# Norms of a two-layer diffusion trunk cut into pieces by tokens, and a weight transpose moved into a projection

## The chip, the cores and the metric

The kernel runs on one core of one Trainium2 chip. A core has five engines that run side by side and meet only at semaphores: TensorE (PE, matrix products), VectorE (DVE), ScalarE (ACT), GpSimdE (POOL) and SyncE (SP), which here only issues DMAs. The metric is the device time of one execution in microseconds.

## The reference

Two blocks of 128 tokens with 1024 features go through two layers: block 0 (the code's t = 0) is a context prompt, block 1 (t = 1) a set of noisy latents. Each block has its own conditioning vector, from which a modulation (shift, scale, gate) is computed for each norm. Cut to what matters here:

```python
h = rms_norm(x, norm_mix[l]) * (1.0 + sc1) + sh1
out = even_mixer(h, ...)             # layer 0: attention and gated DeltaNet
out = odd_mixer(h, ...)              # layer 1:
#   z = gelu(h @ w_in); u, v = split(z)
#   v = layer_norm(v)
#   mixed = einsum("gpq,bnqgc->bnpgc", w_s, v) + b_s
#   out = (u * mixed) @ w_out
x = x + g1 * out
h = rms_norm(x, norm_ffn[l]) * (1.0 + sc2) + sh2
x = x + g2 * hier_moe(h, ...)        # router, then 2 of 32 experts a token
```

All weights are float32 and stream in from HBM: 288 MB are read. `w_s` (the spatial weights) are four 128x128 matrices that mix tokens; the product on PE needs them transposed.

## The kernel before

The residual stream `xT` and the normalised stream `hT` lie with features on the partitions, as [128, 8 tiles, 2 blocks, 128 tokens]. Every engine's program is written out by hand in the order in which it runs, and engines wait on counting semaphores: nothing is scheduled. Weights come in slots of 2 MB, eleven of them (five in `ring`, six in `scratch`, the code's `more`). SP issues the loads in a fixed order; each waits until the slot's previous user is done (`used`, or for one slot `v_mix`, line 668). From the fourth of eleven expert passes on, SP must also know which experts the routing chose (line 703).

**A router norm** (`moe`, lines 1276, 1862 and 2370) goes block by block. DVE adds half of a block's out-projection to `xT` (`residual`, line 2348, four tiles at a time) and signals `v_x`; ACT squares these four tiles (line 1625), signals `a_sq`; PE sums the squares with a product against ones (`mean_square_of`, line 881); ACT takes the root (lines 1617 and 1620); DVE multiplies all eight tiles of the block by it (line 2378) and signals `v_xn`. Then DVE modulates tiles 0 to 3 (line 2069) and ACT tiles 4 to 7 (line 1630). PE waits for both (`h_ready`, line 889) and runs the router products (line 1286). For block 0 all of this lies beside the out-projection of block 1; for block 1 there is little else for PE.

**The norm ahead of layer 1's in-projection** (`norm`, lines 1638 and 2073) takes both blocks at once and is cut by tiles: DVE normalises tiles 0 to 3 of both blocks (line 2085, 1024 columns), DVE modulates them for block 0 while ACT does for block 1; then the same with tiles 4 to 7. The in-projection on PE first computes v, block 0 with all eight tiles, then block 1 (line 1536); its first product waits for the first half, its fifth tile for the second.

**The spatial weights** are loaded by ACT's DMA queue behind that norm (line 1956, with three more small loads). PE transposes them (line 1557) after the last u product of the in-projection (line 1549), ACT copies the result to `wsT` (line 1980) after its last gelu and a table load (`roots()`), and PE mixes (line 1563) when the copy (`a_ws`) and the layer norm (`v_ln`) are there. DVE follows each quarter of the mixing with an addition and a product (lines 2680 and 2682), and the out-projection (line 1262) waits for the first two.

## Time and profile before

| | |
|---|---|
| median of three timed runs | 843.4 us (842.76 to 843.53) |
| profiled execution, its own time | 846.99 us |
| its span | 845.0 us |
| PE busy | 785.5 us, 93% |
| DVE / ACT busy | 321.5 / 166.5 us |
| DMA | 291.47 MB, mean 345 GB/s, hardware queue 87.3% of 16 engines' span |
| mean granted PE clock | 0.973 |

The span is what the profiler saw of the core's work; the time of the execution is 2.0 us longer. Times in the views count from the span's start. Durations below all come from this one execution. A matmul in float32 appears as two PE instructions, so that sixteen products of 128x128 read as x32. The granted clock is a share of full speed: 1.00 or 0.50.

### The profile page before, as it was taken

Reading aid. Unit: us, or ns where it says so; the run is one execution under the profiler, and the core shown is the slowest. Engines: PE = TensorE matmul, PEld = TensorE weight load, DVE = VectorE, ACT = ScalarE, POOL = GpSimd, SP = SyncE. Lnnn points to the kernel's source line nnn. Section 1 sums busy time; section 2 is a strip of 40 time slices with the busy share of each in tenths; the row PEclk is TensorE's granted clock in tenths of the full one; section 3 lists DMA queues with packets and bytes.
Section 4 is the critical chain, followed back from the end, with each engine's and each line's share of the span. In section 5 each row is a group of like instructions: output and inputs, shape, how many; then the busy total and the mean of one; then the engine's idle time right before and its main releaser. Section 6 shows DMA issues by size and latency. Waiting matters only on the chain.

```text
span 845.0 us, 15981 instructions
## 1 busy us (share of the span) xinstructions
PE 785.5 (93%) x6910; PEld 524.4 (62%) x6910; DVE 321.5 (38%) x687; ACT 166.5 (20%) x323; POOL 12.3 (1%) x17
## 2 busy tenths in 40 slices
PE   3999999998999999999977989989999999998697
PEld 3788568677898655556542444679865545664244
DVE  1155467653414433433332340223353344333224
ACT  3112411323203111111100141040321111111013
POOL 0000001020000000000000000000000000000000
PEclk9999999999999999999998999999999999999798
DMA  9999779493899599999999999996549999999993
GB/s 342 387 371 386 254 261 353 147 344 104 274 390 399 222 414 363 362 417 415 420 415 411 400 387 385 389 409 243 200 147 417 384 361 417 416 419 415 413 402 144
DMA packets 97879, 291.47 MB, mean 345 GB/s; under 512 B 11833, under 2 KB 14991, under 8 KB 87567
## 3 DMA queue, kind: packets, MB, share of 16 engines
q1 hardware_dynamic: 86960, 284.32, 87.3%
q10 hardware_dynamic: 10847, 6.11, 2.5%
q8 instruction: 56, 0.92, 0.4%
q14 instruction: 16, 0.13, 0.0%
HBM read 288.30 MB, written 2.10 MB: 344 GB/s over the span
## 4 chain that ended last, share of the span: by engine, by line
PE 74%; SPq 11%; DMA 7%; DVE 2%; ACT 2%; issue 2%; ACTq 1%; DVEq 0%
PE psum L1360 7%; PE psum L1262 7%; PE psum L905 7%; PE psum L1335 6%; PE psum L1345 6%; PE psum L1392 5%; PE psum L858 5%; PE psum L965 5%; DMA scratch<-in_w_exp_up 5%; SPq L742 5%; PE psum L1536 4%; PE psum L1549 3%; PE psum L1403 3%; SPq L761 2%; PE psum L1027 2%
## 5 line engine op out<-in xcount | busy, mean ns | idle before, releaser
L1345 PE MATMUL psum<-scratch,hT 128*32 128x512 f32 (+1 forms) x384 | 77.0, 647 | 16.5 <-DMA ring<-in_w_exp_up 8.7
L1335 PE MATMUL psum<-scratch 128*128 128x128 f32 x704 | 82.9, 276 | 0.9 <-DVE scratch L2478 0.9
L1335 PEld LDWEIGHTS psum<-scratch 128*128 128x128 f32 x704 | 80.5, 192 | 1.3 <-issue 1.2
L1345 PE MATMUL psum<-ring,hT 128*32 128x512 f32 (+1 forms) x288 | 67.7, 619 | 5.1 <-DMA scratch<-in_w_exp_up 5.1
L905 PE MATMUL psum<-hT,ring 128*128 128x256 f32 x256 | 57.8, 383 | 1.1 <-DVE hT L2069 0.7
L1403 PEld LDWEIGHTS psum<-const,scratch 128*128 128x128 bf16 x480 | 45.1, 97 | 21.5 <-issue 13.6
L1403 PE MATMUL psum<-const,scratch 128*128 128x256 bf16 x480 | 55.9, 272 | 1.5 <-DVE scratch L2494 1.5
L1345 PEld LDWEIGHTS psum<-scratch,hT 128*32 128x32 f32 (+1 forms) x384 | 21.0, 122 | 54.1 <-issue 54.1
L905 PEld LDWEIGHTS psum<-hT,ring 128*128 128x128 f32 x256 | 47.9, 190 | 9.6 <-DVE hT L2069 2.0
L2487 DVE TENSOR_SCALAR hT<-psum,const 128x512 f32<-128x512 f32 x22 | 16.5, 751 | 95.1 <-PE psum L1392 93.6
L1903 ACT ACTIVATE scratch<-psum 128x256 f32<-128x256 f32 x22 | 8.4, 383 | 211.4 <-PE psum L1345 124.8
L1360 PE MATMUL psum<-scratch,hT 128*64 128x512 f32 (+1 forms) x208 | 42.7, 594 | 0.6 <-DMA scratch<-in_w_exp_up 0.6
L965 PE MATMUL psum<-ring,hT 128*128 128x512 f32 x96 | 42.6, 597 | 0.0
L2498 DVE TENSOR_TENSOR scratch<-psum,scratch 128x256 f32<-128x256 f32 x22 | 9.3, 425 | 84.3 <-ACT scratch L1903 84.3
L858 PE MATMUL psum<-ring,condT 128*2 128x128 f32 x1280 | 40.4, 282 | 0.0
L1392 PE MATMUL psum<-scratch,const 128*32 128x512 f32 (+2 forms) x248 | 40.1, 596 | 0.0
L858 PEld LDWEIGHTS psum<-ring,condT 128*2 128x2 f32 x1280 | 32.5, 88 | 7.4 <-issue 4.1
L1345 PEld LDWEIGHTS psum<-ring,hT 128*32 128x32 f32 (+1 forms) x288 | 17.9, 118 | 30.4 <-issue 30.4
L1360 PE MATMUL psum<-ring,hT 128*64 128x512 f32 (+1 forms) x176 | 35.7, 594 | 0.8 <-DMA ring<-in_w_exp_up 0.8
L1392 PE MATMUL psum<-ring,const 128*32 128x512 f32 (+2 forms) x216 | 32.8, 596 | 0.0
L1536 PE MATMUL psum<-ring,hT 128*128 128x512 f32 x64 | 29.7, 624 | 2.2 <-ACT hT L1630 2.2
L965 PEld LDWEIGHTS psum<-ring,hT 128*128 128x128 f32 x96 | 17.8, 190 | 20.8 <-issue 20.7
...
## 6 DMA issues: line engine op xcount, KB each, us to landing
...
```

What stands on the lines that cost most here:

```text
L742: sp.dma_start(slot(s)[:, at:at + 1024], w[e][:, 1024 * kh:1024 * kh + 1024]).then_inc(full[s], 16)
L858: last = mm(bank[mbank[g]][32 * m:32 * m + NB, at:at + P], condT[:, :, k], w[:, k, m * P:(m + 1) * P], start=(k == 0), stop=(k == KT - 1))
L905: last = mm(out[:, c2 * T:(c2 + 1) * T], w[:, k, m * P:(m + 1) * P], hT[:, k, :, :], start=(k == 0 and k1 == KT), stop=(k == k1 - 1), skip ...
L965: last = mm(bank[b], hT[:, k, t, :], w[:, k, :], start=(k == 0), stop=(k == KT - 1))
L1262: last = mm(bank[2 * t + m // 4][:, (m % 4) * P:(m % 4 + 1) * P], w[m // 4][:, k, (m % 4) * P:(m % 4 + 1) * P], hT[:, k, t, :], start=(k = ...
L1335: last = mm(bank[b][:, k * P:(k + 1) * P], hrow[:, t, half * 4 + k, :], Pm[:, t, :], start=(t == 0), stop=(t == 1))
L1345: last = mm(bank[0][i * m:(i + 1) * m, :], xg[:, k, i * m:(i + 1) * m], w[e][:, k, :, :], start=(k == 0), stop=(k == KT - 1))
L1360: last = mm(bank[0][i * m:(i + 1) * m, :], xg[:, 4 * kh + k, i * m:(i + 1) * m], w[i // 2][:, i % 2, k, :, :], start=(kh == 0 and k == 0), ...
L1392: last = mm(bank[1 + half][i * m:(i + 1) * m, :], hidT[:, a, i * m:(i + 1) * m], slot(slots[e // 2])[:, base:base + 512], start=(a == 0), ...
L1403: last = mm(bank[4 + k // 2][:, (k % 2) * T:(k % 2 + 1) * T], y3[:, j, k, :], ohT, start=False, stop=True, skip_group_check=True)
L1536: last = mm(bank[4 + 2 * j + t], hT[:, k, t, :], w[:, k, :], start=(k == 0), stop=(k == KT - 1))
L1549: last = mm(bank[b][:, (m % 2) * T:(m % 2 + 1) * T], w[:, k, m * P:(m + 1) * P], hT[:, k, :, :], start=(k == 0), stop=(k == KT - 1))
```

## The change

There are three parts. The norms are cut by tokens and tiles: in `norm` DVE normalises four tiles of one block (512 columns), four times, and each engine modulates two of these four tiles, DVE the first two and ACT the last two; in `moe` the block's normalisation becomes two of 512 columns, tiles 4 to 7 (ACT's) first. The last half of the residual of block 1 is signalled twice, after two tiles and after four; ACT squares each pair by itself and PE waits for each. The transposes of the spatial weights stand on PE in front of the second u chunk of the in-projection, and ACT's copy ahead of the gelu of that chunk. The counts of the semaphores follow (`SQ0`, `H0`).

```diff
@@ -79,7 +79,8 @@
 MOE_SLOTS = PASS_AT[NPASS]
 
 
-SQ0 = [None, None, 0, 4, 8, 12]
+SQ0 = [None, None, 0, 5, 9, 14]
+H0 = [None, 0, 2, 4, 8]
 MS0 = [None, None, 0, 2, 3, 5]
 
 
@@ -881,15 +882,15 @@
             def mean_square_of(n, sq, b, t):
 
                 for k in range(KT):
-                    if k % 4 == 0:
-                        pe.wait_ge(S.a_sq, SQ0[n] + 2 * t + k // 4 + 1)
+                    if k in (0, 4) or (t == 1 and k == 6):
+                        pe.wait_ge(S.a_sq, SQ0[n] + 2 * t + (0, 0, 1, 2)[k // 2] + 1)
                     last = mm(bank[b][:, t * P:(t + 1) * P], ones, sq[:, k, t * P:(t + 1) * P], start=(k == 0), stop=(k == KT - 1))
                 last.then_inc(S.t_ms, 1)
 
             def h_ready(n, i):
 
-                pe.wait_ge(S.v_h, 2 * (n - 1) + i + 1)
-                pe.wait_ge(S.a_h, 2 * (n - 1) + i + 1)
+                pe.wait_ge(S.v_h, H0[n] + i + 1)
+                pe.wait_ge(S.a_h, H0[n] + i + 1)
 
             mod_chunk(0, 0)
             mod_chunk(0, 2)
@@ -1531,8 +1532,8 @@
                 w = slot_kn(s)
                 for t in range(NB):
                     for k in range(KT):
-                        if j == 0 and t == 0 and k % 4 == 0:
-                            h_ready(3, k // 4)
+                        if j == 0 and k % 4 == 0:
+                            h_ready(3, 2 * t + k // 4)
                         last = mm(bank[4 + 2 * j + t], hT[:, k, t, :], w[:, k, :], start=(k == 0), stop=(k == KT - 1))
                     if t == 0:
                         last.then_inc(S.t_v, 1)
@@ -1543,6 +1544,11 @@
                 w = slot_kn(s)
                 if j == 1:
                     pe.wait_ge(S.v_mod, M_B + 1)
+                    pe.wait_ge(S.ld_router, 16 * 10)
+                    pe.wait_ge(S.a_gv, 4)
+                    for g in range(4):
+                        last = nc.tensor.transpose(bank[4][:, g * P:(g + 1) * P], wsp[:, g, :], ident)
+                    last.then_inc(S.t_ws, 1)
                 for m in range(4):
                     b = 2 * j + m // 2
                     for k in range(KT):
@@ -1551,11 +1557,6 @@
                     if m == 1:
                         last.then_inc(S.t_u, 1)
                 used(last)
-            pe.wait_ge(S.ld_router, 16 * 10)
-            pe.wait_ge(S.a_gv, 4)
-            for g in range(4):
-                last = nc.tensor.transpose(bank[4][:, g * P:(g + 1) * P], wsp[:, g, :], ident)
-            last.then_inc(S.t_ws, 1)
             pe.wait_ge(S.a_ws, 1)
             for t in range(NB):
                 pe.wait_ge(S.v_ln, t + 1)
@@ -1638,9 +1639,10 @@
             def norm(n, b, l, shift):
 
                 root_mean(n, b, 0, NB)
-                for half in range(2):
-                    act.wait_ge(S.v_xn, 2 * (n - 2) + half + 1)
-                    modulate(n, l, shift, 4 * half, 4 * half + 4, 1)
+                for t in range(NB):
+                    for half in range(2):
+                        act.wait_ge(S.v_xn, 4 * (n - 2) + 2 * t + half + 1)
+                        modulate(n, l, shift, 4 * half + 2, 4 * half + 4, t)
 
             def mod_row(g):
 
@@ -1862,11 +1864,11 @@
             def moe(l):
                 n = 2 * l + 2
                 for t in range(NB):
-                    for half in range(2):
-                        act.wait_ge(S.v_x, 4 * l + 2 * t + half + 1)
-                        squares(n, sqm, 4 * half, 4 * half + 4, t, t + 1)
+                    for i, (k0, k1) in enumerate([(0, 4), (4, 8)] if t == 0 else [(0, 4), (4, 6), (6, 8)]):
+                        act.wait_ge(S.v_x, 5 * l + 2 * t + i + 1)
+                        squares(n, sqm, k0, k1, t, t + 1)
                     root_mean(n, 5, t, t + 1)
-                    act.wait_ge(S.v_xn, 2 * (n - 2) + t + 1)
+                    act.wait_ge(S.v_xn, 4 * (n - 2) + 2 * t + 1)
                     modulate(n, l, 3 * KT, 4, KT, t)
                 tokens_rows(l, 0)
                 tokens_rows(l, 1)
@@ -1975,9 +1977,9 @@
                 A(uT[:, 2 * b:2 * b + 2, :].rearrange("p k n -> p (k n)"), bank[b], ACT.Gelu_apprx_tanh).then_inc(S.a_gelu, 1)
                 if b == 1:
                     layer_norm_scale()
+                    act.wait_ge(S.t_ws, 1)
+                    A(wsT[:, :, :].rearrange("p g n -> p (g n)"), bank[4], ACT.Copy).then_inc(S.a_ws, 1)
             roots()
-            act.wait_ge(S.t_ws, 1)
-            A(wsT[:, :, :].rearrange("p g n -> p (g n)"), bank[4], ACT.Copy).then_inc(S.a_ws, 1)
 
             moe(1)
             moe_experts(1)
@@ -2074,17 +2076,17 @@
 
                 dve.wait_ge(S.a_rstd, MS0[n] + 2)
                 dve.wait_ge(S.v_a, 4)
-                for half in range(2):
-                    k = 4 * half
-                    normalise(k)
-                    dve.wait_ge(S.v_xn, 2 * (n - 2) + half + 1)
-                    modulate(n, l, shift, k, k + 4, 0)
-
-            def normalise(k):
-
-                V.tensor_tensor(hT[:, k:k + 4, :, :].rearrange("p k t n -> p k (t n)"),
-                                xT[:, k:k + 4, :, :].rearrange("p k t n -> p k (t n)"),
-                                bcast_mid(rstd[:, :], 4), ALU.mult).then_inc(S.v_xn, 1)
+                for t in range(NB):
+                    for half in range(2):
+                        k = 4 * half
+                        normalise(t, k)
+                        dve.wait_ge(S.v_xn, 4 * (n - 2) + 2 * t + half + 1)
+                        modulate(n, l, shift, k, k + 2, t)
+
+            def normalise(t, k):
+
+                V.tensor_tensor(hT[:, k:k + 4, t, :], xT[:, k:k + 4, t, :],
+                                bcast_mid(rstd[:, t * P:(t + 1) * P], 4), ALU.mult).then_inc(S.v_xn, 1)
 
             dve.wait_ge(S.v_xt, 3)
             for half in range(2):
@@ -2357,6 +2359,8 @@
                     for m in range(4 * half, 4 * half + 4):
                         last = V.scalar_tensor_tensor(xT[:, m, t, :], bank[2 * t + half][:, (m % 4) * P:(m % 4 + 1) * P],
                                                       modT[:, l * MT + 2 * KT + m, t:t + 1], xT[:, m, t, :], ALU.mult, ALU.add)
+                        if t == 1 and m == 5:
+                            last.then_inc(S.v_x, 1)
                     last.then_inc(S.v_x, 1)
 
             def add_scaled(src, b, at):
@@ -2375,8 +2379,9 @@
                     residual(["out0", "out1"][l], l, t)
                     dve.wait_ge(S.a_rstd, MS0[n] + t + 2)
                     dve.wait_ge(S.v_a, 5)
-                    V.tensor_tensor(hT[:, :, t, :], xT[:, :, t, :], bcast_mid(rstd[:, t * P:(t + 1) * P], KT), ALU.mult).then_inc(S.v_xn, 1)
-                    dve.wait_ge(S.v_xn, 2 * (n - 2) + t + 1)
+                    normalise(t, 4)
+                    normalise(t, 0)
+                    dve.wait_ge(S.v_xn, 4 * (n - 2) + 2 * t + 2)
                     modulate(n, l, 3 * KT, 0, 4, t)
                 dve.wait_ge(S.t_lg, 2 * l + 2)
                 link(V.tensor_tensor(lg, bank[0][:, 0:72].rearrange("p (t n) -> p t n", t=2),
```

The norm ahead of the in-projection on DVE, before (`hT<-xT,rstd` is a normalisation, `hT<-hT,mulA,modT` a modulation of one tile of one block, L2059 the modulation vectors of the next norm):

```order
L2085 TENSOR_TENSOR hT<-xT,rstd 128x1024 [waits v_a,a_rstd]
L2069 TENSOR_SCALAR hT<-hT,mulA,modT 128x128 [waits v_xn]
L2069 TENSOR_SCALAR hT<-hT,mulA,modT 128x128 x3
L2085 TENSOR_TENSOR hT<-xT,rstd 128x1024
L2069 TENSOR_SCALAR hT<-hT,mulA,modT 128x128 [waits v_xn]
L2069 TENSOR_SCALAR hT<-hT,mulA,modT 128x128 x3
L2059 TENSOR_TENSOR modT<-psum,cols 128x16 [waits t_mod]
```

The same norm on DVE in the change, in which L2088 is the normalisation and L2071 the modulation:

```order
L2088 TENSOR_TENSOR hT<-xT,rstd 128x4x128 [waits v_a,a_rstd]
L2071 TENSOR_SCALAR hT<-hT,mulA,modT 128x128 [waits v_xn]
L2071 TENSOR_SCALAR hT<-hT,mulA,modT 128x128
L2088 TENSOR_TENSOR hT<-xT,rstd 128x4x128
L2071 TENSOR_SCALAR hT<-hT,mulA,modT 128x128 [waits v_xn]
L2071 TENSOR_SCALAR hT<-hT,mulA,modT 128x128
L2088 TENSOR_TENSOR hT<-xT,rstd 128x4x128
L2071 TENSOR_SCALAR hT<-hT,mulA,modT 128x128 [waits v_xn]
L2071 TENSOR_SCALAR hT<-hT,mulA,modT 128x128
L2088 TENSOR_TENSOR hT<-xT,rstd 128x4x128
L2071 TENSOR_SCALAR hT<-hT,mulA,modT 128x128 [waits v_xn]
L2071 TENSOR_SCALAR hT<-hT,mulA,modT 128x128
```

Two normalisations of 1024 columns with four modulations each have become four of 512 with two each; the first modulation stands behind half of the columns.

The end of the in-projection on PE, before (`hT,ring` and `hT,scratch` are the two u chunks, `const,scratch` the transposes against the identity, L1563 the mixing):

```order
L1549 MATMUL psum<-hT,ring 128x256 [waits slot_full2]
L1549 MATMUL psum<-hT,ring 128x256 x31
L1549 MATMUL psum<-hT,scratch 128x256 [waits v_mod,slot_full10]
L1549 MATMUL psum<-hT,scratch 128x256 x31
L1557 MATMUL psum<-const,scratch 128x128 [waits a_gv,ld_router]
L1557 MATMUL psum<-const,scratch 128x128 x3
L1563 MATMUL psum<-scratch 128x128 [waits v_ln,a_ws]
L1563 MATMUL psum<-scratch 128x128 x7
L1563 MATMUL psum<-scratch 128x128 [waits v_ln]
L1563 MATMUL psum<-scratch 128x128 x7
L1262 MATMUL psum<-hT,scratch 128x128 [waits slot_full9,v_mix,a_gelu]
```

The same stretch of PE in the change, in which L1550 is the transpose, L1555 the u product and L1564 the mixing:

```order
L1555 MATMUL psum<-hT,ring 128x256 [waits slot_full2]
L1555 MATMUL psum<-hT,ring 128x256 x31
L1550 MATMUL psum<-const,scratch 128x128 [waits ld_router,a_gv,v_mod,slot_full10]
L1550 MATMUL psum<-const,scratch 128x128 x3
L1555 MATMUL psum<-hT,scratch 128x256 x32
L1564 MATMUL psum<-scratch 128x128 [waits v_ln,a_ws]
L1564 MATMUL psum<-scratch 128x128 x7
L1564 MATMUL psum<-scratch 128x128 [waits v_ln]
L1564 MATMUL psum<-scratch 128x128 x7
L1263 MATMUL psum<-hT,scratch 128x128 [waits slot_full9,v_mix,a_gelu]
```

The four transposes, with their waits for ACT's small loads (`ld_router`) and for the last gelu of v (`a_gv`), have moved ahead of the 32 products of the second chunk; the mixing now stands directly behind these.

ACT in the same place, before (L1975 is the gelu of u, L1980 the copy):

```order
L1951 ACT_TABLE_LOAD
L1975 ACTIVATE scratch<-psum 128x512 [waits t_u]
L1975 ACTIVATE scratch<-psum 128x512 [waits used]
L1596 ACT_TABLE_LOAD
L1980 ACTIVATE scratch<-psum 128x512 [waits t_ws]
L1625 ACTIVATE scratch<-xT 128x4x128 [waits v_x] x2
```

The same stretch of ACT in the change, in which L1977 is the gelu and L1981 the copy:

```order
L1953 ACT_TABLE_LOAD
L1981 ACTIVATE scratch<-psum 128x512 [waits t_ws]
L1977 ACTIVATE scratch<-psum 128x512 [waits t_u]
L1977 ACTIVATE scratch<-psum 128x512 [waits used]
L1597 ACT_TABLE_LOAD
L1626 ACTIVATE scratch<-xT 128x4x128 [waits v_x] x2
```

The copy has moved from behind the last gelu and a table load to a place ahead of the third gelu.

## Rows read from the trace of the kernel before

**Rows 1.** The page, part 4: the chain that ended last, shares of the span by engine.
```profile
PE 74%; SPq 11%; DMA 7%; DVE 2%; ACT 2%; issue 2%; ACTq 1%; DVEq 0%
```

**Rows 2.** The chain in order of time (start us, us, what), its two longest DMA pieces.
```profile
465.79 15.35 DMA scratch<-in_w_exp_up
...
803.97 15.62 DMA ring<-in_w_exp_up
```

**Rows 3.** Windows: engines' busy us (count), granted clock, DMA share, GB/s; before each expert stage.
```profile
275.00:283.00 8.00, 7.06 (x117) 6.34 (x110) 6.17 (x33) 1.87 (x3) 0.00 (x0) 1.00 0.02 7
...
610.00:620.00 10.00, 9.13 (x158) 7.98 (x162) 6.81 (x39) 3.73 (x7) 0.00 (x0) 0.83 0.01 3
```

**Rows 4.** Timeline, first router norm (start us, us, engine line op out<-in xcount [idle <-releaser]).
```profile
252.94 1.95 PE L886 MATMUL psum<-scratch,const 128*128 128x128 f32 x16
...
262.72 2.35 PE L886 MATMUL psum<-scratch,const 128*128 128x128 f32 x16
...
265.85 1.23 DVE L2378 TENSOR_TENSOR hT<-xT,rstd 128x1024 f32<-128x1024 f32 x1 [2.65 <-ACT rstd L1620]
...
267.11 1.65 ACT L1630 ACTIVATE hT<-hT,modT,mulA 128x128 f32<-128x128 f32 x4 [1.29 <-DVE hT L2378]
267.11 1.12 DVE L2069 TENSOR_SCALAR hT<-hT,mulA,modT 128x128 f32<-128x128 f32 x4
...
268.91 2.13 PE L1286 MATMUL psum<-wrt,hT 128*128 128x36 f32 x16 [0.47 <-ACT hT L1630]
```

**Rows 5.** Timeline, norm ahead of the in-projection and the in-projection's two v halves.
```profile
502.45 1.23 DVE L2085 TENSOR_TENSOR hT<-xT,rstd 128x1024 f32<-128x1024 f32 x1 [3.37 <-ACT rstd L1620]
503.72 1.65 ACT L1630 ACTIVATE hT<-hT,modT,mulA 128x128 f32<-128x128 f32 x4 [1.29 <-DVE hT L2085]
...
505.51 15.67 PE L1536 MATMUL psum<-ring,hT 128*128 128x512 f32 x32 [2.19 <-ACT hT L1630]
...
522.97 14.00 PE L1536 MATMUL psum<-ring,hT 128*128 128x512 f32 x32
```

**Rows 6.** Line 697, loads issued at 485.6 and 488.1: first in-projection chunk, issue to landing.
```profile
DMA to landing us min/median/max: 12.6/14.3/16.1
```

**Rows 7.** Lines 2682 and 1630, every instruction (ns min/median/max, first and last start).
```profile
L2682 DVE TENSOR_TENSOR hT<-hT,scratch x4: 691/692/693, 570.3 to 574.5; 128x512 f32<-128x512 f32 x4
...
L1630 ACT ACTIVATE hT<-hT,modT,mulA x32: 477/478/496, 23.2 to 609.5; 128x128 f32<-128x128 f32 x32
```

**Rows 8.** Timeline, between the in-projection and the out-projection of layer 1.
```profile
565.47 1.28 ACT L1596 ACT_TABLE_LOAD   x1
566.76 0.60 ACT L1980 ACTIVATE scratch<-psum 128x512 f32<-128x512 f32 x1
...
567.41 5.47 PE L1563 MATMUL psum<-scratch 128*128 128x128 f32 x32 [2.16 <-ACT scratch L1980]
569.56 0.69 DVE L2680 TENSOR_TENSOR hT<-psum,scratch 128x512 f32<-128x512 f32 x1 [8.77 <-PE psum L1563]
...
572.72 21.61 PE L1262 MATMUL psum<-hT,scratch 128*128 128x128 f32 x192
```

**Rows 9.** Windows of one microsecond: granted clock is the third number from the end.
```profile
500.00:501.00 1.00, 1.00 (x6) 0.89 (x5) 0.00 (x0) 0.00 (x0) 0.00 (x0) 1.00 1.05 385
506.50:507.50 1.00, 1.00 (x2) 0.34 (x1) 0.62 (x3) 1.00 (x3) 0.00 (x0) 0.50 1.05 387
567.50:568.50 1.00, 1.00 (x5) 1.00 (x6) 0.00 (x0) 0.00 (x0) 0.00 (x0) 0.50 1.07 426
...
767.00:768.00 1.00, 1.00 (x12) 0.31 (x8) 0.97 (x2) 0.00 (x0) 0.00 (x0) 1.00 1.00 401
```

**Rows 10.** Timeline of PE, a short and a longer wait elsewhere.
```profile
499.36 2.10 PE L878 MATMUL psum<-scratch,const 128*128 128x256 f32 x9 [0.97 <-issue]
...
766.31 0.59 PE L1345 MATMUL psum<-scratch,hT 128*32 128x512 f32 x1 [2.42 <-DMA ring<-in_w_exp_up]
```

**Rows 11.** Line 1959, the last of ACT's four small loads, issued at 507.5: issue to landing.
```profile
DMA to landing us min/median/max: 12.1/12.1/12.1
```

## The prediction

> **What bounds the kernel now.** I read the chain of waits first: PE holds 74% of it, SP's DMA issues 11%, DMA 7% [rows 1]. Which share matters where shows in the same chain in order of time: its long DMA pieces stand at the end of the two expert stages, to 481.1 and to 819.6 [rows 2]. So an expert stage ends when its weights have landed, 2 MB slot after slot. The next question is what starts that stream. The windows ahead of both expert stages answer it: from 275 to 283 the DMA engines are 2% busy, from 610 to 620 1% [rows 3]. Every slot is full there, and no load goes out until routing has chosen experts or PE has freed a slot. An expert stage is therefore a block of nearly fixed length that starts when routing ends, and a microsecond saved ahead of routing is saved at the end, in PE's part of the block and in DMA's. The edits all lie ahead of one or both of these points, so I read the timeline there for what PE waits for.
>
> **1. Router norms (in both layers), second block of tokens.** PE runs the second mean square as 16 instructions in 2.35 us, where the first took 1.95 with nothing to wait for; then DVE normalises 1024 columns in 1.23, ACT's four modulations take 1.65 and DVE's four 1.12, and PE starts the router products 1.80 us after both engines began, having sat idle 0.47 [rows 4].
> - With the residual half signalled after two tiles, ACT squares 256 columns twice instead of 512 once. PE reaches tile 4 at about 263.6, when the first pair is there, and the last pair comes before tile 6: the mean square should cost 1.95, so 0.40 is saved.
> - A normalisation of 512 columns takes 0.69 by the nearest row, an operation of the same shape and operand kinds [rows 7]. ACT can start after the first: 0.69 instead of 1.23, and would end 0.54 earlier. DVE now has 0.69 + 0.69 + 1.12 = 2.50 where it had 1.23 + 1.12 = 2.35, so DVE ends last. The pass was 1.23 + 1.65 and gaps = 2.91 (265.85 to 268.76); it becomes 2.50 and gaps of 0.05 = 2.55. Saved: 0.36.
> - PE itself could start the router products 0.47 + 0.40 = 0.87 earlier at most; the sum of 0.76 lies inside that. I take 0.75 a layer, **1.5 in all**. Bounds: 0.35 a layer if the two short normalisations eat the second part, 0.87 if they overlap.
>
> **2. Norm ahead of the in-projection.** Before, PE waits 2.19 us: DVE normalises four tiles of both token blocks (502.45, 1.23), then ACT's four modulations of block 1 run 503.72 to 505.37, and PE starts at 505.51 although its first products read block 0 alone [rows 5]. After: 0.69 for 512 columns, then two modulations on each engine; ACT's take 0.48 + 0.39 (its four take 1.65, so 0.39 apart) = 0.87. Ready at 502.45 + 0.69 + 0.04 + 0.87 = 504.05, PE at 504.2: 1.31 earlier. What is late next? The second half of the first weight chunk was issued at 488.1 and took 16.1 us, so it landed at 504.2 [rows 6]; the two nearly tie. I take **1.2**. The later pieces are ready one per 1.3 us or so (0.69 + 0.60), while PE needs 3.5 for each, and stay covered. Bounds: 0.9 (landing a little late) to 1.31.
>
> The Trainium skill, page "VectorE: DVE Perf Modes", section "The TRN2 errata — SBUF-src ops pay a fixed extra latency per instruction", speaks against pieces: many small operations pay a fixed cost each. The trace shows it: 2 x 0.69 against 1.23, 0.15 for each split [rows 5, 7]. By that rule alone, with DVE's total deciding, this norm would end 0.3 us later and the router norms 0.15; the trace puts DVE's total on the path only in the router norms, where it is in my sum.
>
> **3. The clock after that wait.** The in-projection's first 32 matmuls took 15.67 us, the next 32 of the same shape 14.00 [rows 5]; at 506.5 the granted clock was 0.50, that is 1.2 instead of 2.4 GHz [rows 9]. It fell right after the wait of 2.19. A wait of 0.97 just before left it at 1.00 [rows 9, 10]. The new wait is 2.19 - 1.2 = 1.0. So I count 15.67 - 14.00 = **1.65** as saved. Bounds: 0 and 1.67.
>
> **4. Spatial weights.** Before, ACT has a table load (1.28) and then the copy (0.60) between the last in-projection product and the mixing; PE is idle 2.16 [rows 8]. Now both transposes and copy happen about ten microseconds earlier, in a stretch where PE is busy and ACT idle; the four transposes cost PE the same wherever they stand. PE goes on at once: **2.1**. The mixing then took 5.47 for 32 instructions at clock 0.50, again after a wait over 2 us [rows 8, 9]; at the out-projection's pace (21.61 for 192, 0.113 each) it is 3.6, 1.85 less. But DVE follows each quarter with two operations of 0.69 [rows 7, 8]: first quarter done about 1.25 after the start, then four operations with gaps, 2.85, then 0.15 to PE: the out-projection starts 4.25 after the mixing instead of 572.72 - 567.41 = 5.31. So the clock gives **1.05** here, bounds 0 and 1.7. The moved-up transposes wait for four small loads issued by ACT at 506 to 507.5; the last landed 12.1 later, at 519.6 [rows 11], over 25 us before PE asks.
>
> **Sum.** 1.5 + 1.2 + 1.65 + 2.1 + 1.05 = 7.5 us. The profiled execution took 847.0 (span 845.0 and 2.0 around it), so it would take 839.5. The three timed runs had a median of 843.4, 3.6 shorter; the saved waits are compute waits and should be in those too, so I subtract the same: **835.9**.
>
> **The rivals.**
> - *Waits go, the clock gives nothing* (it does not fall in the timed runs, or falls elsewhere after the change). For: the timed runs are 3.6 shorter than the profiled one, about what two clock drops cost; and after a wait of 2.42 at 766.31 the clock was still 1.00 [rows 9, 10]. Against: both waits on these places show it. Without items 3 and the clock part of 4, 7.5 - 2.7 = 4.8: 838.6. Beside it: the Trainium skill, "TensorE: Matmul & The Clock Gate", section "What's actually happening", says that how many matmuls run slow differs from execution to execution of one kernel; by that the 2.7 would be there in some executions and absent in others.
> - *The weights decide in the in-projection.* PE, 2.9 us ahead, meets the landing of its chunks. For: rows 6, a tie already for the first chunk. Against: only this chunk is that close, and its stream itself starts 0.75 earlier. If items 2 and 3 vanish: 7.5 - 2.85 = 4.65, and 838.8.
> - *The expert stream hides all.* If the DMA stream had been full through routing, nothing of this would reach the end: 843.4. The 2% and 1% of rows 3 speak against it.
> - *Slower: a stall inside the second in-projection.* The transposes now stand in front of that projection's second chunk on PE, with 12 us of products, the mixing and everything behind them. If the four small loads land later than about 547, PE stops; each microsecond of lateness costs one, and the clock 1.67 more once the wait is long. It overcomes the 7.5 from about 553 on, 46 us after issue, and at 50 us would give 843.4 - 7.5 + 10.5 + 1.7 = 848. Against: 12.1 us of landing [rows 11], in a stretch where the DMA engines were already saturated.
>
> **How the numbers follow.** Forecast 0.62 (own range 834.4 to 837.4: half of each bound), clock gives nothing 0.20, weights decide 0.08, stream hides all 0.04, stall 0.03, and 0.03 for more than the sum, where the clock also stays up in the first router stage. A difference of 0.2%, 1.7 us, is about what can be told from none. Faster by more than that: 0.62 + 0.20 + 0.08 + 0.03 = 0.93, of which I give back 0.02 for small sums going wrong together: 0.91. Within: 0.05. Slower: 0.04. The range runs from 834.0 (all upper bounds) to 840.0 (waits alone, with the lower bounds of 1 and 2).
>
> **What would show it.** Router norm: mean square of block 1 in about 1.95, first normalisation to router products 2.7 instead of 3.1, DVE ending last. In-projection: a wait near 1.0, the first 32 matmuls in 14.0 at clock 1.00. Mixing: directly behind the in-projection, about 4 us at clock 1.00, with DVE releasing the out-projection. Idle DMA engines still ahead of both expert stages, and the stages' lengths unchanged. Wrong: a clock of 0.5 in either place, an in-projection released by DMA, expert stages that grow by what was saved ahead of them.

## The result, and the profile after

| | before | changed |
|---|---|---|
| median of the timed runs beside each other, us | 843.66 (7 runs, 842.76 to 851.66) | 838.33 (7 runs, 834.74 to 843.53) |
| profiled execution, us | 847.0 | 837.6 |
| its span, us | 845.0 | 835.8 |

The ratio of the runs beside each other is 0.9924, with a 95% interval of 0.9897 to 0.9951: 6.4 us faster, 4.1 to 8.7. (The two medians differ by 5.3.) The kernel is faster, by less than 1%. The forecast was 835.9 and its range 834.0 to 840.0. The profiled pair differs by 9.4, more than the timed runs. So two questions are open after the result: do the five steps stand, and why do the two differences not agree?

The changed kernel, page part 4, shares of the chain by engine. It answers to [rows 1].

```profile
PE 72%; SPq 14%; DMA 7%; issue 2%; DVE 2%; ACTq 1%; ACT 1%; DVEq 0%
```

The changed kernel, windows: us, then busy us (count) of PE, PEld, DVE, ACT, POOL, granted clock, DMA share, GB/s. The first answers to [rows 3], the other three to [rows 9].

```profile
275.00:283.00 8.00, 6.62 (x67) 6.04 (x68) 6.57 (x35) 1.93 (x4) 0.00 (x0) 1.00 0.02 6
...
501.50:502.50 1.00, 1.00 (x3) 0.38 (x2) 0.96 (x3) 0.64 (x3) 0.00 (x0) 1.00 1.04 385
559.00:560.00 1.00, 1.00 (x11) 1.00 (x11) 0.23 (x1) 0.98 (x2) 0.00 (x0) 1.00 1.01 406
609.00:610.00 1.00, 1.00 (x25) 0.79 (x16) 0.88 (x5) 0.00 (x0) 0.00 (x0) 0.50 0.00 0
```

The balance of the program is as it was, the DMA engines still idle (2%) ahead of the first expert stage. The clock is 1.00 one microsecond into the in-projection and into the mixing, where it was 0.50. The last row shows a stretch at half clock inside the second routing. The kernel before had one in that routing too (0.83 on the mean from 610 to 620 [rows 3]), but in another place, as shown further down.

The changed kernel, timeline of the first router norm, second block of tokens (start us, us, engine line op out<-in xcount [idle before <-releaser]). It answers to [rows 4]; L887 is the mean square, L2088 the normalisation, L1631 and L2071 the modulation, L1287 the router products.

```profile
263.26 2.05 PE L887 MATMUL psum<-scratch,const 128*128 128x128 f32 x16
...
266.09 1.29 DVE L2088 TENSOR_TENSOR hT<-xT,rstd 128x512 f32<-128x512 f32 x2 [2.35 <-ACT rstd L1621]
266.82 1.65 ACT L1631 ACTIVATE hT<-hT,modT,mulA 128x128 f32<-128x128 f32 x4 [0.76 <-DVE hT L2088]
...
267.42 1.12 DVE L2071 TENSOR_SCALAR hT<-hT,mulA,modT 128x128 f32<-128x128 f32 x4
...
268.61 1.98 PE L1287 MATMUL psum<-wrt,hT 128*128 128x36 f32 x16
```

The mean square takes 2.05 instead of 2.35. From the start of the normalisation to the router products it is 2.52 (266.09 to 268.61) instead of 3.06 [rows 4]. DVE ends last, at 268.54. The two short normalisations back to back take 1.29 together.

The changed kernel, timeline of the norm ahead of the in-projection. It answers to [rows 5]; L1537 is the v product.

```profile
498.78 0.69 DVE L2088 TENSOR_TENSOR hT<-xT,rstd 128x512 f32<-128x512 f32 x1 [3.37 <-ACT rstd L1621]
499.51 0.88 ACT L1631 ACTIVATE hT<-hT,modT,mulA 128x128 f32<-128x128 f32 x2 [0.76 <-DVE hT L2088]
...
500.69 14.00 PE L1537 MATMUL psum<-ring,hT 128*128 128x512 f32 x32 [1.04 <-DMA ring<-in_w_in_odd]
```

And its chain of waits in order of time, DMA pieces only (start us, us, what), to set beside [rows 2]:

```profile
398.85 25.32 DMA scratch<-in_w_exp_up
...
484.58 16.06 DMA ring<-in_w_in_odd
```

PE waits 1.04 instead of 2.19. ACT's modulations end at 500.39, and what releases PE is the first weight chunk, landing at 484.58 + 16.06 = 500.64. The first 32 products take 14.00 instead of 15.67.

The changed kernel, timeline from the transposes (L1550) to the out-projection (L1263). It answers to [rows 8]; L1981 is the copy, L1564 the mixing.

```profile
544.36 0.60 PE L1550 MATMUL psum<-const,scratch 128*128 128x128 f32 x4
...
550.59 0.60 ACT L1981 ACTIVATE scratch<-psum 128x512 f32<-128x512 f32 x1
...
558.61 3.73 PE L1564 MATMUL psum<-scratch 128*128 128x128 f32 x32
...
562.43 0.68 DVE L2685 TENSOR_TENSOR hT<-psum,scratch 128x512 f32<-128x512 f32 x1
562.62 8.61 PE L1263 MATMUL psum<-hT,scratch 128*128 128x128 f32 x75 [0.27 <-issue]
```

The mixing follows the in-projection with no wait and takes 3.73 instead of 5.47; the out-projection starts 4.01 after it instead of 5.31.

**Where the 9.2 us of span went.** I compared the starts of the same PE instructions in the two traces; from the start of one stage to that of the next the changed kernel is shorter by: 0.91 up to the first expert stage (a gain of 1.45 less 0.54 by which it had started later), **2.76 inside the first expert stage**, 1.15 up to the in-projection, 1.67 in its first 32 products, 2.31 up to the mixing, 1.30 up to the out-projection; **0.79 longer** from there to the second expert stage, and 0.1 more lost to the end. The two in bold are in no step of the prediction. The first is in a stage that no edit touches; for the second, the router norm saved 0.8 there and something took 1.6. The gain of 1.45 ahead of the first expert stage is not the router norm's alone either: from the second mean square to the gather, the product that collects the experts' tokens (L1335), the five unedited traces that kept full clock up to there took 15.7 to 16.1 us and the six with both router edits 15.2. The edits give 0.6 there, and the other 0.8 is the clock, which fell in the kernel before and not in the changed one.

### The profile page after: what moved, and what is told of

Its sections match the earlier page's. It is cut to its first block, busy times and chain, and to the rows that moved or that the text cites. A ratio compares the mean times of both kernels' runs of the same rounds, so it can differ in the third digit from the quotient of the medians.

```text
span 835.8 us, 15991 instructions
## 1 busy us (share of the span) xinstructions
PE 780.8 (93%) x6910; PEld 521.6 (62%) x6910; DVE 322.0 (39%) x693; ACT 167.0 (20%) x325; POOL 12.3 (1%) x17
## 4 chain that ended last, share of the span: by engine, by line
PE 72%; SPq 14%; DMA 7%; issue 2%; DVE 2%; ACTq 1%; ACT 1%; DVEq 0%
PE psum L1361 7%; PE psum L1263 7%; PE psum L906 7%; PE psum L1336 6%; PE psum L1346 6%; PE psum L1393 5%; PE psum L966 5%; PE psum L859 5%; SPq L743 5%; PE psum L1537 3%; PE psum L1555 3%; PE psum L1404 3%; DMA scratch<-in_w_exp_up 3%; PE psum L1028 2%; DMA ring<-in_w_in_odd 2%
## 5 line engine op out<-in xcount | busy, mean ns | idle before, releaser
L1336 PE MATMUL psum<-scratch 128*128 128x128 f32 x704 | 83.8, 277 | 0.9 <-DVE scratch L2483 0.9
L1336 PEld LDWEIGHTS psum<-scratch 128*128 128x128 f32 x704 | 81.3, 194 | 1.5 <-issue 1.4
L1404 PEld LDWEIGHTS psum<-const,scratch 128*128 128x128 bf16 x480 | 45.1, 97 | 21.4 <-issue 13.6
L906 PEld LDWEIGHTS psum<-hT,ring 128*128 128x128 f32 x256 | 47.8, 190 | 9.6 <-DVE hT L2071 2.0
L966 PE MATMUL psum<-ring,hT 128*128 128x512 f32 x96 | 42.6, 596 | 0.0
L859 PE MATMUL psum<-ring,condT 128*2 128x128 f32 x1280 | 40.3, 280 | 0.6 <-issue 0.6
L859 PEld LDWEIGHTS psum<-ring,condT 128*2 128x2 f32 x1280 | 32.6, 87 | 7.6 <-issue 5.2
L1263 PEld LDWEIGHTS psum<-hT,ring 128*128 128x128 f32 x256 | 28.8, 192 | 0.7 <-issue 0.7
```

The source lines that it names most:

```text
L859: last = mm(bank[mbank[g]][32 * m:32 * m + NB, at:at + P], condT[:, :, k], w[:, k, m * P:(m + 1) * P], start=(k == 0), stop=(k == KT - 1))
L906: last = mm(out[:, c2 * T:(c2 + 1) * T], w[:, k, m * P:(m + 1) * P], hT[:, k, :, :], start=(k == 0 and k1 == KT), stop=(k == k1 - 1), skip ...
L966: last = mm(bank[b], hT[:, k, t, :], w[:, k, :], start=(k == 0), stop=(k == KT - 1))
L1263: last = mm(bank[2 * t + m // 4][:, (m % 4) * P:(m % 4 + 1) * P], w[m // 4][:, k, (m % 4) * P:(m % 4 + 1) * P], hT[:, k, t, :], start=(k = ...
L1336: last = mm(bank[b][:, k * P:(k + 1) * P], hrow[:, t, half * 4 + k, :], Pm[:, t, :], start=(t == 0), stop=(t == 1))
L1404: last = mm(bank[4 + k // 2][:, (k % 2) * T:(k % 2 + 1) * T], y3[:, j, k, :], ohT, start=False, stop=True, skip_group_check=True)
```

## The experiments

**Table 1** gathers what the traces of all fourteen profiled kernels show at the places in question, each routing from the starts of PE's instructions. "Routing" is from the start of the second mean square to the last four transposes ahead of the experts (L1315 in the kernel before, L1316 in the changed one), which stand 0.5 us before the first expert product. "Low in routing 1" tells where the half clock lay in layer 1's routing: "hidden" where PE then waited for DVE anyway (0.2 us or less was lost), "costs" where it lay behind that wait, over the chunk and the gather that the experts wait for.

| kernel | routing, layer 0 | wait, first 32 of in-projection | wait, mixing | routing, layer 1 | low in routing 1 |
|---|---|---|---|---|---|
| before | 20.94 | 2.19, 15.67 | 2.16, 5.47 | 20.78 | hidden |
| before again (first) | 21.62 | 2.18, 13.97 | 2.16, 3.84 | 20.71 | hidden |
| before again (second) | 22.99 | 2.18, 13.97 | 2.16, 3.84 | 20.70 | hidden |
| residual only | 20.65 | 2.18, 13.97 | 2.16, 5.47 | 20.40 | none |
| router norms only | 23.17 | 2.18, 13.97 | 2.16, 5.46 | 19.90 | none |
| spatial only | 21.61 | 2.19, 15.67 | none, 3.73 | 20.71 | hidden |
| norm only | 23.00 | 0.88, 13.97 | 2.16, 5.39 | 20.91 | hidden |
| before, waits filled | 20.95 | 0.34, 13.97 | 0.31, 3.84 | 20.71 | none |
| norm and spatial | 23.08 | 0.99, 14.00 | none, 3.73 | 23.88 | costs |
| changed | 19.49 | 1.04, 14.00 | none, 3.73 | 21.51 | costs |
| changed again | 21.01 | 1.07, 14.00 | none, 3.73 | 21.51 | costs |
| changed, waits filled | 19.52 | 0.30, 14.00 | none, 3.73 | 19.90 | none |
| changed, whole blocks | 20.90 | 2.19, 13.97 | none, 3.73 | 23.01 | costs |
| changed, late loads | 19.49 | 1.06, 14.00 | none, 3.73 | 21.53 | costs |

### Before again, twice

No edit: the kernel before, once timed and profiled, once profiled alone.

> The kernel before, unchanged, a second time. The two profiled executions differ by 9.2 us, but only 6.9 to 7.0 of it can be read as stretches in front of the expert stages that became shorter; in the first expert stage, which the change does not touch, the landings after about 350 us come 3.6 us earlier while the issues before it are 0.9 earlier, so 2.7 us appear there. Theory A (chance): the 16 DMA engines' skew varies between executions of one kernel, so this repeat may show either state, and its span may differ from 845.0 by up to 3 us. Theory B (the change causes it): the repeat shows the same late landings as the first execution, the weight issued at about 402.5 landing 25.3 us later at 427.8, and a span within 1 us of 845.0.

> The kernel before, unchanged, for one more trace. Theory 1 (whether the clock falls at a wait of 2.2 us differs between executions): over this and the other traces with unchanged waits it falls in some, not in all. Theory 2 (the wait decides): low at both places. The length of the first expert stage should lie between 201 and 205 us and be long where the 16 DMA engines have drifted apart: about 202 at a mean spread of landings under 2 us, 204 at 3 us.

Measured: ratio 1.0003 (0.9978 to 1.0028) and a span of 843.9 for the first; span 843.3 for the second. Timeline of PE in the first:

```profile
505.51 13.97 PE L1536 MATMUL psum<-ring,hT 128*128 128x512 f32 x32 [2.18 <-ACT hT L1630]
...
565.72 3.84 PE L1563 MATMUL psum<-scratch 128*128 128x128 f32 x32 [2.16 <-ACT scratch L1980]
569.83 5.37 PE L1262 MATMUL psum<-hT,scratch 128*128 128x128 f32 x46 [0.27 <-issue]
```

And of PE in the second:

```profile
506.82 13.97 PE L1536 MATMUL psum<-ring,hT 128*128 128x512 f32 x32 [2.18 <-ACT hT L1630]
```

The same program with the same waits, and the clock falls at neither place. So the wait alone does not decide the fall. Where the wait was not shortened, the in-projection ran slow in 2 of 7 traces (before, spatial only) and the mixing in 4 of 6 (before, residual only, router norms only, norm only). With the wait shortened, filled or gone, neither did, in 7 and 8 traces. For the mixing, 4 of 6 against none of 8 is hard to put down to luck; for the in-projection, 2 of 7 against none of 7 can well be luck, so that the shorter wait keeps the clock up there is likely but not shown. What the change removes is a chance, not a fixed price. My estimates from these counts are 1.67 x 2/7 = 0.5 in the in-projection, and 1.2 (5.31 against 4.11 from mixing to out-projection) x 4/6 = 0.8 in the mixing; with so few traces either can be off by half of itself or more.

### One part at a time

Norm ahead of the in-projection alone:

```diff
-                for half in range(2):
-                    k = 4 * half
-                    normalise(k)
...
-                    modulate(n, l, shift, k, k + 4, 0)
+                for t in range(NB):
+                    for half in range(2):
+                        k = 4 * half
+                        normalise(t, k)
...
+                        modulate(n, l, shift, k, k + 2, t)
```

> Only the norm ahead of the in-projection is cut by tokens and tiles; router norms and spatial weights as before. Theory A (the sum of waits and clock): root of the mean square to in-projection 1.9 us instead of 3.1 (1.2 less), the first 32 in-projection matmuls in 14.0 instead of 15.7 at clock 1.00, together 2.8 us of time; the mixing still waits 2.2 and runs at clock 0.50. Rival (the clock drop only moves): 1.2 us of time, with another stretch at 0.50 before the mixing.

Measured: 0.9992 (0.9967 to 1.0018). Its timeline:

```profile
503.07 0.69 DVE L2089 TENSOR_TENSOR hT<-xT,rstd 128x512 f32<-128x512 f32 x1 [3.36 <-ACT rstd L1622]
503.80 0.88 ACT L1632 ACTIVATE hT<-hT,modT,mulA 128x128 f32<-128x128 f32 x2 [0.76 <-DVE hT L2089]
...
504.82 13.97 PE L1538 MATMUL psum<-ring,hT 128*128 128x512 f32 x32 [0.88 <-ACT hT L1632]
```

Here ACT releases PE and the wait is 0.88, 1.31 less than 2.19: the upper bound of the step. In the changed kernel the weights came last and it was 1.15. The tie was priced rightly from both sides. A gain of 1.3, and a chance of 0.5 more, lies inside the interval.

Spatial weights alone:

```diff
                 if j == 1:
                     pe.wait_ge(S.v_mod, M_B + 1)
+                    pe.wait_ge(S.ld_router, 16 * 10)
+                    pe.wait_ge(S.a_gv, 4)
+                    for g in range(4):
+                        last = nc.tensor.transpose(bank[4][:, g * P:(g + 1) * P], wsp[:, g, :], ident)
+                    last.then_inc(S.t_ws, 1)
```

> Only transposes and copy of the spatial weights are moved. Theory A: no wait ahead of the mixing, the mixing in about 3.7 at clock 1.00, out-projection 3.7 us earlier against the end of the in-projection: 3.7 us of time. Rival (DVE's two operations a quarter hold the out-projection back as before): 2.2 us of time. The wait of 2.2 and the clock 0.50 stay at the in-projection.

Measured: 0.9975 (0.9946 to 1.0005), 2.1 us by the ratio; the interval, up to 4.6, holds both theories. The in-projection in its timeline:

```profile
502.29 15.67 PE L1536 MATMUL psum<-ring,hT 128*128 128x512 f32 x32 [2.19 <-ACT hT L1630]
```

In this trace the clock did fall at the untouched wait. The mixing is that of the changed kernel, and from the 32nd v product to the mixing it takes 43.92 instead of 46.23: the 2.31 of this step come from this edit.

Router norms alone (normalisation in two pieces, residual half signalled twice):

```diff
-                    V.tensor_tensor(hT[:, :, t, :], xT[:, :, t, :], bcast_mid(rstd[:, t * P:(t + 1) * P], KT), ALU.mult).then_inc(S.v_xn, 1)
+                    for k in (4, 0):
+                        V.tensor_tensor(hT[:, k:k + 4, t, :], xT[:, k:k + 4, t, :],
+                                        bcast_mid(rstd[:, t * P:(t + 1) * P], 4), ALU.mult).then_inc(S.v_xn, 1)
...
+                        if t == 1 and m == 5:
+                            last.then_inc(S.v_x, 1)
```

> Only the router norms: normalisation in two pieces and the residual's last half signalled twice; both layers. Theory A: second mean square in 2.05 instead of 2.35, first normalisation to router products 2.5 instead of 3.1, 0.84 us a layer, 1.7 us of time. Theory B (it is this part that brings the 2.7 us in the first expert stage's landings): 4 us or more of time. Rival (the idle DMA ahead of the expert stages means nothing): 0.

Measured: 0.9987 (0.9966 to 1.0007), at most 2.9 us, which rules out theory B. And with the signal alone (the last three lines of that diff and the waits that belong to them):

> The kernel before with the last residual half signalled twice only. Theory A: second mean square 2.05 instead of 2.35, so 0.3 us a layer, 0.6 in all, which no timing here can tell from none (ratio 0.999). Rival: nothing changes, since the normalisation waits for something else; then the stretch from the first mean square to the gather stays 16.37 us in layer 1. Also one more trace in which the waits ahead of in-projection and mixing are those of before: if the clock there falls by chance, it falls in one, both or neither; if the wait decides, in both.

Measured: 0.9972 (0.9951 to 0.9992). Table 1 separates the two: routing in layer 1 is 20.71 before, 20.40 with the signal alone, 19.90 with both. So the signal gives 0.31 and the normalisation in pieces 0.50, together 0.81 in layer 1. In layer 0 the router products start 0.84 earlier as well, but only 0.6 of it is left at the gather: inside the modulation chunk between them PE then stands 0.57 to 0.63 for something that the trace does not name, against 0.17 to 0.68 in the five unedited traces. The timing of the signal-only kernel, 2.4 us by the ratio, is more than its edit can give by its own trace (0.3 in each layer, 20.65 against 20.94 in layer 0); its interval ends at 0.7 us. Single parts of a microsecond cannot be read off these timings, only off the traces.

Norm and spatial together, and the whole change once more:

> The changed kernel without its router-norm edits (residual halves signalled once, router norms in 1024 columns). Theory A: 1.15 + 2.4 of waits and 1.6 of clock = 5.1 us, ratio 0.994. Theory B (a gain ahead of the second expert stage needs the router edits too, or is taken back by low clock elsewhere): 3.4 us or less, ratio 0.996 or more. Trace: second mean square 2.35 and last norm to gather as before, in-projection and mixing as in the changed kernel.

> The changed kernel once more, beside its parts. By the traces so far: waits 1.15 (in-projection) + 2.4 (spatial weights) + 0.8 a router norm (1.6) = 5.1 us that every execution keeps, and the clock, which in unchanged places fell ahead of the in-projection in 2 of 4 traces (1.65 each) and ahead of the mixing in 3 of 4 (1.3 each), so 1.6 on average. Theory A (these add up): ratio 0.992, 6.7 us. Theory B (the parts do not add up to more than their medians showed, 0.2 + 3.2 + 0.2): ratio 0.9955 or more. In its trace the waits ahead of in-projection and mixing are 1.0 and none, and both stages run at full clock.

Measured: 0.9934 (0.9913 to 0.9954) without the router norms, 0.9929 (0.9903 to 0.9955) with everything, side by side; medians 840.82 and 841.38 against 845.55. Both intervals end at 0.9955 or below, which speaks against the theory that only 3.6 us are there. By their points the two large edits give 5.6 together and 0.7 + 2.1 alone; each has an uncertainty near 2, so the timings don't settle whether they add. The traces do: in the norm, the in-projection and the mixing the combined kernels show the waits and lengths of the single ones. The second routing is the exception, and the next section is about it. What the router norms save cannot be seen between these two timings.

### Where 1.6 us were lost again: the two routings

The second routing of the changed kernel, timeline of PE. L859 is a modulation chunk of the next stage, L1301 the first of the routing's transposes, L1336 the gather:

```profile
602.07 1.93 PE L859 MATMUL psum<-scratch,condT 128*2 128x128 f32 x64
606.26 0.63 PE L1301 MATMUL psum<-scratch,const 128*128 128x32 f32 x4 [2.26 <-DVE scratch L2420]
...
607.64 2.66 PE L859 MATMUL psum<-scratch,condT 128*2 128x128 f32 x61
610.23 2.90 PE L1336 MATMUL psum<-scratch 128*128 128x128 f32 x16
```

The kernel before had its low stretch earlier:

```profile
611.96 1.95 PE L1291 MATMUL psum<-const,hT 128*128 128x128 f32 x8
613.84 2.60 PE L858 MATMUL psum<-scratch,condT 128*2 128x128 f32 x64
617.18 0.63 PE L1300 MATMUL psum<-scratch,const 128*128 128x32 f32 x4 [0.73 <-DVE scratch L2415]
...
618.56 1.91 PE L858 MATMUL psum<-scratch,condT 128*2 128x128 f32 x61
620.39 2.05 PE L1335 MATMUL psum<-scratch 128*128 128x128 f32 x16
```

Before, PE's work ahead of L1300 was slow (1.95 for eight products that take 1.07 in the changed kernel, 2.60 for a chunk that takes 1.93), but DVE was later still, and PE waited 0.73 for it: the half clock cost next to nothing (20.78 against the 20.71 of the same kernel with its waits filled, which kept full clock there). In the changed kernel that work ran at full clock, PE waited 2.26 for DVE instead, and the low stretch came behind the wait, over the second chunk (2.66 instead of 1.91) and the gather (2.90 instead of 2.05), where nothing hides it: 1.6 us. The edits did not make this wait: it is 2.25 to 2.27 in every trace that reaches it at full clock without products put into it, with the router edits or without them. The kernel before with its other two waits filled shows it:

```profile
613.59 0.63 PE L1300 MATMUL psum<-scratch,const 128*128 128x32 f32 x4 [2.27 <-DVE scratch L2417]
```

Again the wait does not decide alone. This trace, router norms only and residual only stood 2.26 or 2.27 there and kept full clock, while all five other traces with the norm by tokens and the moved transposes lost 1.6 (three times) or 3.1 (twice; one of them is norm and spatial, which has no router edit, and the other is whole blocks). To test it I put idle products into that wait (and three into the wait of 1.0 ahead of the in-projection):

```diff
                 else:
                     mod_chunk(1, 10)
+                    idle_products(6, 8)
...
             mod_chunk(1, 4)
+            idle_products(6, 3)
             for j in range(2):
```

> The changed kernel with three products of zeros in the wait in front of the in-projection and eight behind the first modulation chunk of layer 1's router stage, where PE waits 2.3 us for the routing and where the granted clock was 0.50 from 608.7 to 612.1. Theory A: clock 1.00 there, the last modulation products and the first gather 1.6 us shorter, 1.6 us less than the changed kernel. Rival (the products end too late or the clock falls elsewhere in the stage): 0 to 0.5 us.

Measured: 0.9924 (0.9897 to 0.9951), median 838.38. Its timeline of PE:

```profile
606.47 1.92 PE L1250 MATMUL psum<-zeros 32*128 32x512 bf16 x8
608.79 0.63 PE L1302 MATMUL psum<-scratch,const 128*128 128x32 f32 x4 [0.41 <-DVE scratch L2422]
...
610.17 1.91 PE L859 MATMUL psum<-scratch,condT 128*2 128x128 f32 x61
612.01 2.05 PE L1337 MATMUL psum<-scratch 128*128 128x128 f32 x16
```

The trace shows the 1.6 back (routing 19.90). The timing does not: it can't be told from the changed kernel (0.9924 and 0.9929). The first expert stage of its trace was 2.3 us longer than in the changed kernel.

**The first routing** has the same trouble, and nothing was edited to test it. The granted clock fell there in 11 of the 14 traces. In three (before, residual only, before with waits filled) it fell early, over the transposes and the modulation chunk:

```profile
270.84 1.95 PE L1291 MATMUL psum<-const,hT 128*128 128x128 f32 x8
272.71 4.25 PE L858 MATMUL psum<-ring,condT 128*2 128x128 f32 x128
```

In eight it fell later, behind a wait of 0.94 to 1.04 for DVE, over the gathers. The second repeat of the kernel before shows it:

```profile
278.95 2.68 PE L1335 MATMUL psum<-scratch 128*128 128x128 f32 x16 [0.94 <-DVE scratch L2478]
...
282.30 3.78 PE L1335 MATMUL psum<-scratch 128*128 128x128 f32 x16
```

A gather takes 2.02 or 2.05 at full clock. In the changed kernel, its twin with waits filled and its twin with late loads the clock stayed up, and the routing took 19.49 to 19.52; where it fell in kernels with the same router edits it took 20.90, 21.01 and 23.17, so 1.4 to 3.7 us more. All three traces with full clock are of the changed kernel or its variants, but so are two with the fall. The mean over the seven traces with unedited router norms is 22.03, over the six with both router edits 20.60: 1.4 less, of which 0.6 are the waits. The rest, 0.8, has an uncertainty of about 1.4, so it can be luck.

The idle products were also tried on the kernel before, with eight idle products in each of its two waits:

```diff
             mod_chunk(1, 4)
+            idle_products(6, 8)
...
             last.then_inc(S.t_ws, 1)
+            idle_products(6, 8)
             pe.wait_ge(S.a_ws, 1)
```

> The kernel before, with eight products of zeros on PE in each of the two waits (in front of the in-projection and in front of the mixing); both waits stay as long. Theory A (the clock falls because PE is idle in the wait, and costs by itself): clock 1.00 in both places, first 32 in-projection matmuls in 14.0 instead of 15.7, mixing in 3.7 instead of 5.5 with the out-projection 1.3 earlier: 2.9 us of time. Rival (the clock falls for another reason, or its cost is hidden behind DVE and DMA): at most 0.5 us.

Measured: 0.9992 (0.9977 to 1.0008), so 0.7 us, at most 1.9. Its waits are 0.34 and 0.31, the starts of both stages unchanged and the clock full in both. If both falls of [rows 9] happened in every execution, this kernel would have gained 1.65 + 1.2 = 2.9. That is outside the interval; 0.5 + 0.8 = 1.3 is inside.

### What the pieces and the early loads are worth

The changed kernel, with the in-projection's norm by whole blocks of 1024 columns, four modulations on each engine:

```diff
-                    for half in range(2):
-                        k = 4 * half
-                        normalise(t, k)
-                        dve.wait_ge(S.v_xn, 4 * (n - 2) + 2 * t + half + 1)
-                        modulate(n, l, shift, k, k + 2, t)
+                    V.tensor_tensor(hT[:, :, t, :], xT[:, :, t, :], bcast_mid(rstd[:, t * P:(t + 1) * P], KT), ALU.mult).then_inc(S.v_xn, 1)
+                    dve.wait_ge(S.v_xn, XN0[n] + t + 1)
+                    modulate(n, l, shift, 0, 4, t)
```

> The changed kernel, but the norm ahead of the in-projection goes by whole blocks: 1024 columns of block 0, then DVE modulates tiles 0 to 3 and ACT tiles 4 to 7. Theory A (token order brings nothing without the smaller pieces): root to in-projection 1.27 + 1.65 + 0.15 = 3.1 us as before the change, the wait about 2.2, and the clock falls again: 2.8 us longer than the changed kernel. Rival (taking block 0 first is what counts): 1.9 us as in the changed kernel.

One execution took 843.3 us. Its timeline:

```profile
500.80 1.23 DVE L2080 TENSOR_TENSOR hT<-xT,rstd 128x1024 f32<-128x1024 f32 x1 [3.22 <-ACT rstd L1622]
502.06 1.11 DVE L2071 TENSOR_SCALAR hT<-hT,mulA,modT 128x128 f32<-128x128 f32 x4
502.06 1.65 ACT L1632 ACTIVATE hT<-hT,modT,mulA 128x128 f32<-128x128 f32 x4 [1.29 <-DVE hT L2080]
...
503.86 2.38 PE L1538 MATMUL psum<-ring,hT 128*128 128x512 f32 x5 [2.19 <-ACT hT L1632]
```

The wait is 2.19 again, 1.15 longer than in the changed kernel. The clock did not fall behind it, as theory A had it (13.97 for the first 32); about half of the 5.6 us by which this execution was longer than the profiled one of the changed kernel (837.6) is clock lost in the two routings, 1.4 and 1.5 (Table 1). Going by token blocks alone does not shorten the wait; the gain is that the first product needs 512 columns and two modulations, not 1024 and four.

The changed kernel, with ACT's four small loads issued after the first gelu of u:

```diff
-            act.dma_start(wsp[:, :, :], I["w_spatial"][0].rearrange("g p q -> p g q")).then_inc(S.ld_router, 16)
...
+                if b == 0:
+                    act.dma_start(wsp[:, :, :], I["w_spatial"][0].rearrange("g p q -> p g q")).then_inc(S.ld_router, 16)
```

> The changed kernel with ACT's four small loads (spatial weights, their bias, the layer norm's gain and bias) issued behind the first gelu of u, 35 us later. They land about 12 us after issue, at 550, where PE asks for them at 544.4. Theory A: PE waits about 6 us inside the in-projection, the clock falls, and the time grows by 6 to 8 us, all of it reaching the end. Rival (the loads land within 6 us or the expert stream hides the stall): less than 1 us.

One execution took 851.0 us, 12.6 more than the changed kernel's median. Timeline of PE:

```profile
530.31 13.98 PE L1555 MATMUL psum<-hT,ring 128*128 128x256 f32 x64
555.72 1.09 PE L1550 MATMUL psum<-const,scratch 128*128 128x128 f32 x4 [11.43 <-DMA scratch<-in_sgu_ln_b]
556.60 15.60 PE L1555 MATMUL psum<-hT,scratch 128*128 128x256 f32 x64
```

This is the slower rival, made to happen. The last load was issued at 538.9 and landed 16.6 later; PE stood 11.43, the clock fell, and the transposes and the next 64 products took 0.49 + 1.62 more than at full clock. The stretch from the in-projection's 32nd product to the mixing grew by 13.7. In the changed kernel these loads land after 8.1 to 13.6 us, the last at 518.3, and PE asks at 544.4: a cushion of 26 us.

### The expert stages: a length that chance sets

Nothing was edited for this; the fourteen traces are the experiment. The first expert stage, from the end of the routing as in Table 1 to where its last combinations begin (L1374 in the kernel before), takes 201.0 to 203.8 us, the second 200.9 to 203.8. I took, for each of the last 72 of a stage's 96 expert loads, the time between the first and the last of the landing steps of its 16 DMA engines, and the mean of these:

| spread of landings, us | stages | length of the stage, us |
|---|---|---|
| under 2.0 | 6 of the first, 7 of the second | 201.0 to 202.8 and 200.9 to 201.2 |
| 2.0 to 2.5 | 4 and 5 | 201.4 to 203.3 and 202.2 to 202.9 |
| over 2.5 | 4 and 2 | 203.3 to 203.8 and 203.3 to 203.8 |

The correlation is 0.89 in the first stage and 0.96 in the second; a microsecond of spread goes with 2.0 and 2.3 of length. In the profile of the kernel before, one of the 16 engines falls behind near 350 us and stays so: about every second load then takes 4.1 to 4.6 from its first to its last landing, against 1.9 in the changed kernel. The chain shows the effect: the same load waits 25.29 us there,

```profile
402.49 25.29 DMA scratch<-in_w_exp_up
```

and 25.32 in the changed kernel, but begins 3.64 earlier (398.85), of which 0.91 was brought in. A load counts as landed when the slowest engine is done. The repeat of the kernel before shows the spread (3.11) and the length (203.8) again, its second repeat does not (1.87; 202.8), and the changed kernel with idle products has it (2.79; 203.3): it goes with the execution, not with the edit. That the spread causes the length was not tested by an experiment, and what makes one engine fall behind stays open.

## Why the prediction was right, and where it was not

1. **Router norms, 1.5 predicted: right.** 0.81 in layer 1 and 0.6 in layer 0, 1.4 in all. Within the 0.81, the mean square gave 0.31 and not 0.40 (2.05, not 1.95), and the normalisation 0.50 and not 0.36. The step said that DVE would hold two times 0.69; back to back they take 1.29. The 0.69 is what one costs when it stands alone. The Trainium skill, page "VectorE: DVE Perf Modes", section "The TRN2 errata — SBUF-src ops pay a fixed extra latency per instruction", charges every instruction; here two pieces cost 0.06 more than the whole (1.29 against 1.23), not 0.15.
2. **Wait ahead of the in-projection, 1.2 predicted: right.** 1.15 with the weights last, 1.31 with ACT last.
3. **Clock after that wait, 1.65: the size in one execution was right, the mean was not.** 1.67 in the profiled pair, but the fall is there in 2 of 7 traces. The term should have been multiplied by a chance: about 0.5.
4. **Spatial weights, 2.1 and 1.05.** The edit gave 2.31, of which 2.16 are the wait; the other 0.15 are the end of the transposes, which take 0.60 with PE idle behind them and 0.43 (544.36 to 544.79) with the next product following. The clock gave 1.30 in this pair and would be 0.8 on average (4 of 6). That DVE limits was right: 4.01 at full clock, 4.25 predicted.
5. **Not in the sum: 1.6 given back in the second routing.** The prediction asked what would be late next, not where else the clock falls. At full clock PE waits 2.26 for DVE's routing chain in this place, before the change as after it (2.27 in the kernel before with filled waits). In five of the six traces that have the moved transposes and the norm by tokens the low stretch lay behind that wait; in the sixth idle products filled it. Whether the edits make this fall likelier, or five in five were luck beside none in the three other traces with that wait, is open.
6. **Not in the sum: the first routing.** The clock fell there in 11 of 14 traces and cost 1.4 to 3.7 us in the three that can be set beside the changed kernel. In the profiled pair it fell before and not after, which is 0.8 of the 9.4. The prediction had it only as a remark, in its 0.03 for more than the sum.

The steps, each at its mean, give 1.4 + 1.15 + 0.5 + 2.3 + 0.8 = 6.15, less about 1.6 x 5/6 = 1.3 given back: 4.8, or 5.6 if the 0.8 of the first routing is no luck. The two timings of the changed kernel gave 6.4 and 6.0 with intervals of 2 or more on either side, so they fit both. A second way to count takes the clock out. Each run reports its mean granted clock. Over all 79 timed runs of the kernel before it is 0.9759 on average, and the time goes against it (correlation -0.74, 0.59 us for each 0.001). Over the 17 of the changed kernel it is 0.9787: 0.0028 more, 1.6 us. The means differ by 5.8 (845.3 and 839.5), so 4.2 are left for the waits, with an uncertainty of about 0.8; they sum to 1.4 + 1.15 + 2.3 = 4.85. That is an argument and not a test: in the kernel before with filled waits the mean clock was 0.0029 higher than in the runs beside it, and the time only 0.7 us shorter, 1.9 at most. So the waits are shown, and how much of the rest is clock stays open.

So the forecast of 835.9 rested on all of the clock's 2.7 and none given back. The rival "waits go, the clock gives nothing" with 838.6 came nearer to the median of 838.3, and by its own words: the clock falls in some executions, or elsewhere after the change. I gave it 0.20, and it deserved more. That the level came out inside the range is in part luck. The forecast was hung on a median of three runs, 843.4, while the kernel before has medians of 844.6 to 845.6 in the later comparisons; the repeat of the changed kernel has 841.4, outside the range, at nearly the same ratio (0.9929). The ends of the range are also not the sums that they are said to be: the bounds of the steps add up to 8.5 and 3.7, which from 843.4 give 834.9 and 839.7. The Trainium skill, page "TensorE: Matmul & The Clock Gate", section "What's actually happening", says of the slow matmuls at a kernel's start that their number differs between executions of one kernel. These traces show the like inside the kernel (2 of 7, 4 of 6). Its sentence stood in the prediction beside the rival when it should have changed the sum. The profiled 9.4 against 7.5 was no confirmation either: 2.8 of it came from the first expert stage, whose length goes with the spread of landings, 0.8 from the clock in the first routing, and 1.6 were lost in the second.

The other rivals: the weights did decide in the in-projection, but only in the tie that was counted. The expert stream hid nothing: the stages' starts moved by what was saved ahead of them. The stall needs loads that land 26 us later than they did; the products behind them take 14.0 us, not the 12 that the rival speaks of.
